# Router logits computed across in two column groups and turned back; scores of the diagonal chunk blocks alone

## The reference, cut to what matters

```python
scores = jnp.einsum('bhncd,bhnsd->bhncs', q_dec, k_inv)   # inside one chunk of 64
causal = jnp.tril(jnp.ones((CHUNK, CHUNK), dtype=bool))
scores = jnp.where(causal, scores, 0.0)
o_intra = jnp.einsum('bhncs,bhnse->bhnce', scores, vh)
```

```python
group_p = jax.nn.softmax((ht @ w_rg).astype(f32) + b_rg.astype(f32), axis=-1)
e_logit = ((ht @ w_re).astype(f32) + b_re.astype(f32)).reshape(T, N_GROUPS, EXPERTS_PER_GROUP)
```

## Time and profile before

| | |
|---|---|
| median of 3 runs | 1662.14 us (1656.52 to 1665.27) |
| the profiled execution's own time | 1662.17 us |
| its span in the profile | 1660.4 us |
| PE, PEld busy | 1520.1 us (92%), 1106.6 us (67%) |
| DVE, ACT, POOL busy | 1210.6 us (73%), 876.0 us (53%), 367.1 us (22%) |
| granted TensorE clock, mean | 0.954 of full speed |

### The profile page before, as it was taken

One profiled execution on the slowest core, in us unless ns is written; L12 is line 12 of the kernel. 1 busy time (PEld: TensorE's weight loads), 2 busy tenths in 40 slices (PEclk: granted clock), 3 DMA queues, 4 the chain that ended last, 5 costly groups with the idle time before them and its releaser, 6 DMA issues. The chain is left out here.

```text
span 1660.4 us, 23932 instructions
## 1 busy us (share of the span) xinstructions
PE 1520.1 (92%) x7453; PEld 1106.6 (67%) x7455; DVE 1210.6 (73%) x1932; ACT 876.0 (53%) x1534; POOL 367.1 (22%) x396
## 2 busy tenths in 40 slices
PE   4899879999989999999999999658999999999974
PEld 2779754889755889666889565445676677766741
DVE  2587994597975598974698945576788878777837
ACT  3324362324574324563324533356788887878846
POOL 1000000000010000011000011123476667665640
PEclk8899979999999999999999998769999999999996
DMA  9452361332332323332321543469999998889859
GB/s 320 168 185 94 93 260 42 89 102 78 126 102 76 102 79 100 116 113 77 89 89 52 228 127 114 153 228 329 352 295 274 344 262 240 223 243 284 275 109 384
DMA packets 201445, 291.27 MB, mean 175 GB/s; under 512 B 10558, under 2 KB 158171, under 8 KB 201370
## 3 DMA queue, kind: packets, MB, share of 16 engines
q1 hardware_dynamic: 171840, 197.18, 34.8%
q0 software_dynamic: 29360, 92.99, 20.5%
q10 hardware_dynamic: 170, 0.10, 0.0%
HBM read 240.42 MB, written 59.26 MB: 180 GB/s over the span
## 5 line engine op out<-in xcount | busy, mean ns | idle before, releaser
L1038 DVE SCALAR_TENSOR_TENSOR cv<-late_rows,taps,cv 128x512 f32<-128x512 f32 x480 | 321.8, 746 | 0.0
L1962 DVE TENSOR_TENSOR w_rest<-wgu,w_high 128x1024 fp32r<-128x1024 f32 x192 | 233.8, 1221 | 88.9 <-ACT w_high L1885 85.5
L1885 ACT ACTIVATE w_high<-wgu 128x1024 fp32r x192 | 201.7, 1054 | 97.9 <-PE pgu L1830 75.9
L531 PE MATMUL bank<-wo,yT 128*128 128x512 f32 x512 | 226.5, 599 | 3.6 <-ACT hT L736 2.5
L488 PE MATMUL bank<-hT_high,tiles_operand 128*128 128x512 f32 x496 | 197.2, 398 | 1.1 <-DVE logits L1132 1.1
L489 PE MATMUL bank<-hT_operand,tiles_operand 128*128 128x512 f32 x496 | 196.6, 396 | 0.0
L490 PE MATMUL bank<-hT_high,win_operand 128*128 128x512 f32 x496 | 196.6, 396 | 0.0
L531 PEld LDWEIGHTS bank<-wo,yT 128*128 128x128 f32 x512 | 96.7, 192 | 119.7 <-issue 117.7
L1840 PE MATMUL py<-wd,hTe 128*128 x384 | 172.7, 592 | 1.8 <-DVE hTe L1985 0.9
L1828 PE MATMUL pgu<-w_high,x_high 128*128 128x512 f32 x384 | 156.8, 408 | 3.8 <-DVE x_rest L1977 3.8
L1016 DVE TENSOR_TENSOR win_operand<-win,tiles_operand 128x2048 fp32r<-128x2048 f32 x48 | 109.9, 2290 | 58.1 <-ACT tiles_operand L758 58.0
(11 more groups left out here) (389 smaller groups left out, 2846.7 us busy)
## 6 DMA issues: line engine op xcount, KB each, us to landing
win<-w_in_in SPq DMA_DIRECT2D x64, 512.0 KB, 5.2
wgu<-w_gate_in SPq DMA_DIRECT2D x32, 1024.0 KB
wgu<-w_up_in SPq DMA_DIRECT2D x32, 1024.0 KB
wd<-w_down_in SPq DMA_DIRECT2D x32, 1024.0 KB
win<-w_in_in SPq DMA_DIRECT2D x16, 1024.0 KB, 5.1
wo<-w_ada_in POOLq DMA_DIRECT2D x6, 2048.0 KB, 11.2
y_dram<-zeros POOLq DMA_DIRECT2D x17, 512.0 KB, 5.1
tiles<-x_in POOLq DMA_DIRECT2D x16, 512.0 KB, 6.0
```

Source lines behind the costliest of these rows:

```text
L531: last = nc.tensor.matmul(out[:], yT[:, w % 2, k, :], wo[:, k, half * 512:(half + 1) * 512], start=(k == 0), stop=(k == KD - 1))
L1038: ins = V.scalar_tensor_tensor(out=cv[:, j], in0=u[:, j, w:w + T], scalar=tap, in1=cv[:, j], op0=ALU.mult, op1=ALU.add)
L1885: A(w_high[:, QK * q:QK * q + QK, :], c.wgu[:, bass.ds(slot, 1), QK * q:QK * q + QK, :].rearrange("p a k n -> p (a k) n"), ACT.Copy).then_ ...
L1962: V.tensor_tensor(w_rest[:, part, :], c.wgu[:, bass.ds(slot, 1), part, :].rearrange("p a k n -> p (a k) n"), w_high[:, part, :].bitcast(F3 ...
```

## The change

Logits of the tiles w = 2, 3 of block 0, all four of blocks 1 and 2, and w = 0, 1 of block 3 (`across`, 12 of 16 tiles): the router columns become stationary (36 columns) and the token tile moving (128 columns). The eight products alternate between two column groups, so that even k sum up in partitions 0 to 35 of the bank and odd k in partitions 64 to 99. A new ACT step `lsave` copies these 100 x 128 values back to `yt`, and a new PE step `lt` multiplies them, stationary, with a 0/1 matrix of 128 x 36 (`both_rows`), which adds the two halves and turns them to one row per token. DVE's `logit` now waits for `lt`. `both_rows` is made once, in the last tile's slot of `c.logits`, with one more DVE operation in `gains`; `cond_wide` moves by 8 columns for it.

Scores: in place of four products of 128 by 128, eight of 64 by 64, one per head and chunk, in two column groups. The semaphore `score_ready` now counts two per tile.

Lists: `lt` and `lsave` are put in. On PE at the end of blocks 0 to 2, `("r", 3)` goes from behind `("piece", 0)` to in front of it, with `("lt", 2)` between them. On DVE `("x1norm", 3)` goes in front of `("logit", 2)`. On ACT, `("turned", 2)` and `lsave` go in front of `("split", 1)`.

```diff
+        both_rows = c.logits[:, NTILES - 1, :]
+        across = lambda t, w: t < NB - 1 or t == NB - 1 and w < 2
...
             def logits(t, i):
                 pe.wait_ge(rin_ready, 2 * tile_no(t, i) + 2)
                 out = take("l", i, 0, t)
+                if across(t, i):
+                    for k in range(KD):
+                        at = k % 2 * CH
+                        last = nc.tensor.matmul(out[at:at + NR, 0:P], c.wroute[:, k, :], yt[:, i % 2, k * P:(k + 1) * P],
+                                                start=k < 2, stop=k >= KD - 2, skip_group_check=True)
+                        if k >= KD - 2:
+                            last.then_inc(logit_rows, 1)
+                    return
...
+            def turn_logits(t, i):
+                pe.wait_ge(logit_rows_saved, across_before(t, i) + 1)
+                out = place("l", i, 0, t)
+                nc.tensor.matmul(out[:, 0:NR], yt[:, i % 2, 0:P], both_rows, start=True, stop=True).then_inc(logit_ready, 1)
...
                 for h in range(NH):
-                    last = nc.tensor.matmul(pS[:, h * P:(h + 1) * P], ki[:, h, tok], qd[:, h, tok], start=True, stop=True)
-                last.then_inc(score_ready, 1)
+                    for s in range(2):
+                        a, b = i * P + s * CH, h * P + s * CH
+                        last = nc.tensor.matmul(pS[s * CH:(s + 1) * CH, b:b + CH], ki[:, h, a:a + CH], qd[:, h, a:a + CH],
+                                                start=True, stop=True, skip_group_check=True)
+                        if h == NH - 1:
+                            last.then_inc(score_ready, 1)
...
-                     ("y", 3, 0), ("A", 3), ("y", 3, 1), ("B", 3), ("r", 2), ("O", 3), ("l", 2), ("piece", 0),
-                     ("r", 3), ("oT", 2), ("oT", 3), ("l", 3), ("piece", 1)]
+                     ("y", 3, 0), ("A", 3), ("y", 3, 1), ("B", 3), ("r", 2), ("O", 3), ("l", 2), ("r", 3), ("lt", 2), ("piece", 0),
+                     ("oT", 2), ("l", 3), ("oT", 3), ("lt", 3), ("piece", 1)]
...
+            def save_logit_rows(t, w):
+                act.wait_ge(logit_rows, 2 * across_before(t, w) + 2)
+                A(yt[0:CH + NR, w % 2, 0:P], place("l", w, 0, t)[0:CH + NR, 0:P], ACT.Copy).then_inc(logit_rows_saved, 1)
...
-                     ("osq", 3), ("orstd", 3), ("rin", 3), ("split", 1), ("turned", 2), ("turned", 3)]
+                     ("osq", 3), ("orstd", 3), ("rin", 3), ("turned", 2), ("lsave", 3), ("split", 1), ("turned", 3)]
...
-                     ("logit", 2), ("x1norm", 3), ("oms", 3), ("state", 3, 1), ("gateo", 3), ("logit", 3),
+                     ("x1norm", 3), ("logit", 2), ("oms", 3), ("state", 3, 1), ("gateo", 3), ("logit", 3),
```

More of the change, by code:

```diff
@@ L248, in present @@
             return t < NB
-        TILE_WORK = ("y", "r", "l", "ysum", "x1sum", "rin", "ynorm", "x1norm", "logit")
+        TILE_WORK = ("y", "r", "l", "lt", "lsave", "ysum", "x1sum", "rin", "ynorm", "x1norm", "logit")
         NEXT_WORK = ("T", "piece", "xsum", "raw", "high", "split", "xnorm", "input", "rest")
@@ L680, in steps @@
                     else:
-                        {"y": y_half, "r": router_turn, "l": logits, "mean": mean, "var": variance, "A": scores, "B": state_sums,
+                        {"y": y_half, "r": router_turn, "l": logits, "lt": turn_logits, "mean": mean, "var": variance, "A": scores, "B": state_sums,
                          "O": outputs, "oT": turn_outputs}[kind](t, *at)
@@ L913, in _ @@
                      ("high", 2), ("key", 3), ("high", 3), ("x1sum", 2), ("osq", 2), ("ysum", 3), ("rin", 2),
-                     ("x1sum", 3), ("orstd", 2), ("osq", 3), ("orstd", 3), ("rin", 3), ("turned", 2), ("split", 1),
-                     ("turned", 3)]
+                     ("x1sum", 3), ("orstd", 2), ("lsave", 2), ("osq", 3), ("orstd", 3), ("rin", 3), ("turned", 2), ("lsave", 3),
+                     ("split", 1), ("turned", 3)]
             MIDDLE = [("ln", 0), ("xsum", 0), ("xsum", 1), ("ln", 1), ("ln", 2), ("raw", 0), ("end", 0), ("exps", 0), ("xsum", 2),
@@ L919, in _ @@
                      ("end", 3), ("gate",), ("key", 0), ("x1sum", 0), ("ysum", 1), ("key", 1), ("rin", 0), ("osq", 0),
-                     ("high", 0), ("orstd", 0), ("x1sum", 1), ("key", 2), ("turned", 0), ("rin", 1), ("osq", 1),
-                     ("high", 1), ("orstd", 1), ("high", 2), ("split", 0), ("turned", 1), ("ysum", 2), ("x1sum", 2),
-                     ("high", 3), ("osq", 2), ("key", 3), ("orstd", 2), ("ysum", 3), ("rin", 2), ("x1sum", 3),
-                     ("osq", 3), ("orstd", 3), ("rin", 3), ("split", 1), ("turned", 2), ("turned", 3)]
+                     ("high", 0), ("orstd", 0), ("x1sum", 1), ("lsave", 0), ("key", 2), ("turned", 0), ("rin", 1), ("osq", 1),
+                     ("high", 1), ("lsave", 1), ("orstd", 1), ("high", 2), ("split", 0), ("turned", 1), ("ysum", 2), ("x1sum", 2),
+                     ("high", 3), ("osq", 2), ("key", 3), ("orstd", 2), ("ysum", 3), ("rin", 2), ("x1sum", 3), ("lsave", 2),
+                     ("osq", 3), ("orstd", 3), ("rin", 3), ("turned", 2), ("lsave", 3), ("split", 1), ("turned", 3)]
             FINAL = [("ln", 0), ("ln", 1), ("ln", 2), ("end", 0), ("exps", 0), ("sq", 0), ("sq", 1), ("sq", 2), ("sq", 3),
@@ L926, in _ @@
                      ("end", 3), ("gate",), ("key", 0), ("x1sum", 0), ("ysum", 1), ("key", 1), ("rin", 0), ("osq", 0),
-                     ("orstd", 0), ("x1sum", 1), ("key", 2), ("turned", 0), ("rin", 1), ("osq", 1), ("orstd", 1),
+                     ("orstd", 0), ("x1sum", 1), ("lsave", 0), ("key", 2), ("turned", 0), ("rin", 1), ("osq", 1), ("lsave", 1), ("orstd", 1),
                      ("turned", 1), ("ysum", 2), ("x1sum", 2), ("osq", 2), ("key", 3), ("orstd", 2), ("ysum", 3),
@@ L941, in steps @@
                         {"ln": log_forget, "exps": head_exps, "end": end_exp, "sq": squares, "var": variance, "gate": conv_gate,
-                         "ysum": y_sums, "x1sum": x1_sums, "rin": router_in, "key": save_keys, "osq": square_outputs,
+                         "ysum": y_sums, "x1sum": x1_sums, "rin": router_in, "lsave": save_logit_rows, "key": save_keys, "osq": square_outputs,
                          "orstd": outputs_rstd, "turned": save_turned}[kind](t, *at)
@@ L1152, in mask @@
             def mask(t, i):
-                dve.wait_ge(score_ready, t * NT + i + 1)
+                dve.wait_ge(score_ready, 2 * (t * NT + i + 1))
                 V.copy_predicated(c.scoreT[:, i % 2].rearrange("p (h n) -> p h n", h=NH),
@@ L1202, in _ @@
                      ("x1norm", 2), ("bcopy",), ("place", 2), ("oms", 2), ("place", 3), ("mask", 3), ("state", 3, 0),
-                     ("input", 3), ("ynorm", 3), ("logit", 2), ("state", 3, 1), ("x1norm", 3), ("osave", 3),
+                     ("input", 3), ("ynorm", 3), ("state", 3, 1), ("x1norm", 3), ("logit", 2), ("osave", 3),
                      ("gateo", 2), ("oms", 3), ("gateo", 3), ("rest", 1), ("logit", 3)]
@@ L1267, in gains @@
                     mod_chain.step(V.tensor_copy(c.grow[:, r * 512:(r + 1) * 512], bank[r][:]))
+                mod_chain.step(V.tensor_tensor(both_rows, c.ident[:, 0:NR], c.ident[:, CH:CH + NR], ALU.add))
                 dve.wait_ge(row_done, 3)
```

4 lines of the change are left out of this document (3 added, 1 removed), and 8 rows, old and new, of tables (FINAL, FIRST, MIDDLE).

## The result

The changed kernel takes 1670.77 us (median of 7 runs, 1670.10 to 1672.46), the kernel before, measured beside it, 1660.46 us (7 runs, 1655.88 to 1665.27): ratio 1.0061 [1.0048, 1.0073], so 10.3 us slower.

What follows compares the result with a forecast made beforehand. PE, busy 92% of the span, was taken as the bound, each new idle moment paid in full. Terms 3.5 + 2.9 - 0.75 - 0.7 = +4.9 us, +10.9 with the clock, gave 1673 us; range 1660 to 1681.

Steps and rivals of the forecast that it cites:

- Its signs: In the trace after: PE idle 2.5 to 4 us before `r` 3, clock 0.50 behind, scores at 0.7 to 0.9 us.
- Logits product: On PE: 1.81 us falls to 1.0, `lt` adds 0.22; net 0.6 us saved per tile where PE is waited for.
- End of blocks 1 and 2: From `l` 2 to piece 1: PE stalls 2.67 us for `r` 3; piece 1 1.74 us later, twice, +3.5 us.
- End of block 0: Same way with block 0's rows: stall 3.81 us, piece 1 at 308.90 instead of 306.02, +2.9 us.
- Middle: Blocks 1 to 3: `l` 0's saving becomes a wait, `logit` 0 1.0 us late; -0.25 us a block, -0.75 for three.
- Scores: Scores product, 0.89 us before: 0.1 us saved in each of 7 places, 0.7 us saved, ends +2.0 and -1.3.
- Clock: Half-speed stretches behind the three new stalls at block ends: 2.0 us each, +6.0 us; 0 if the clock stays up.
- The code's part: Sum of all terms without the clock: 3.5 + 2.9 - 0.75 - 0.7 = +4.9 us.
- The rival without a stall: Block ends: `xn_ready` of tile 3 comes before `l` 2 is over, no stall, no clock drop; -4.2 us, 1658 us; 12%.

Runs made afterwards that it cites:

- `filled`: The changed kernel plus unread products of 512 columns ahead of `r` 3, four in block 0, three in blocks 1 and 2: 1666.71 us, ratio 1.0041 to before.
- `changed_again`: The changed kernel as it is, run once more: 1669.82 us, ratio 1.0051 to the kernel before.
- `stall_alone`: The kernel before with only `r` 3 moved ahead of piece 0 and `x1norm` 3 ahead of `logit` 2: 1670.67 us, ratio 1.0054 to before.
- `turn_behind`: The changed kernel with `r` 3 back behind piece 0, `lsave` 2 ahead of `x1sum` 3, `logit` 2 ahead of `x1norm` 3: 1660.99 us, ratio 0.9995 to before.
- `block0_filled`: `odd_bank` plus unread products of 128 columns ahead of waits in block 0: 1651.47 us, ratio 0.9945 to the kernel before.
- `odd_bank`: The changed kernel with logits in bank 1 or 3, `r` 3 then `lt` 2 behind piece 0, `logit` 2 behind `gateo` 3: 1652.80 us, ratio 0.9947 to before.

## Why the prediction was right

Forecast +10.9 us, measured +10.3, by the mechanism that it named. Its signs came, with two exceptions: the clock stayed at 1.00 behind one of the three stalls (block 1), and a scores step took 0.62 us and not 0.7 to 0.9. Term by term:

- **Logits product.** 1.0 us forecast, 1.00 measured: eight pairs at 0.11 and some 0.1 for leaving the split array. Right; the two column groups work side by side.
- **End of blocks 1 and 2.** Stall 2.67 forecast, 2.69 measured; `r` 3 0.93 for 0.87; the wait for `logit` 2 0.38 for 0.37. From piece 0 to piece 1 7.94 for 8.13: ACT's copy took 0.26 us, not 0.45, and no wait was left ahead of `lt` 3. Sum +1.60 us (13.29 - 11.69) for +1.74.
- **End of block 0.** Stall 3.83 for 3.81. The end with the clock up is seen in `filled`: block 0 is 112.71 - 109.94 = +2.8 us there with the same half-speed time as before; forecast +2.9.
- **Middle.** The wait ahead of the outputs came (1.14 us for some 0.9), so did `logit` 0's late start (0.90 us for 1.0). A whole block 1 or 2, free of half-speed time, is +1.1 us; the steps' terms add up to 1.74 - 0.25 - 0.1 (two scores places at most 0.2) = +1.3 to +1.4.
- **Scores.** 0.1 us a place forecast, 0.18 measured at the place shown, 0.25 us for a whole block, and nothing in the time. The term was too small to matter either way. The Trainium skill, page TensorE: Matmul & The Clock Gate, Part 3, has weight loads overlap with running products only when the row group differs, by which the scores would have been at their slow end. The trace does not bear that out: both column groups share their rows, and eight pairs took 0.62 us, 0.08 each, less than the 0.11 of a pair with 128 moving columns.
- **Clock.** 2.0 us for each of three stalls forecast, from stretches of 3.3 and 10.1 us taken at half their length. In the ledger before has 45.9 us at half speed, after 58.9 and, run again, 58.8: 13 us more, at 0.42 us each 5.4 us, for 6.0. The sum was right and its places were not: behind the stalls it was 6.8, 0 and 6.8 us in one execution and 3.4 us behind each of the three in the other. That 6.0 was met so closely is luck in part. In the three executions with such stalls (after, `changed_again`, `stall_alone`) eight of nine stalls had a half-speed stretch behind them; of the same places in before, `turn_behind` and `filled`, where PE had no such stall, none did. So the idle time is what does it, though not every time.

The code's part, with 2.8 for block 0, 1.1 twice and -0.3 for block 3 up to its third logits product, is +4.7 us for the +4.9 forecast. With the clock's 5.4 that makes 10.1, near the 10.3 of the medians; the profiled execution is only 8.5 us longer, because its block 3 came out 1.0 us shorter behind that product with no less time at half speed, which stays unexplained. The rival without a stall was closest to what could have been: `turn_behind`, which has none, came out level and not at -4.2, for two short waits at each block end took the stall's place, one of them for the same bank, and the scores brought less than they had been given. What the prediction did not look for is that this bank stood in the way of the order that pays.

## What to carry to other kernels

A cheaper product needs a place where PE is what is waited for; moving a step ahead of a long one to make room for it trades a hidden dependency for a stall, and in eight of nine such stalls here PE paid twice, once in the stall's length and once in clock. Price the move by the end of the releasing engine's operation, before pricing the product. When a wait goes back to a shared PSUM bank, try another bank before another order: here two lines for the bank, with `r` 3 in its old place and `lt` 2 and `logit` 2 moved back, turned +10 us into -8.8.

## What had not been expected of the hardware

- Going into a split array costs 0.09 us ahead of the first product, as coming back does behind the last.
- A stretch of 3.4 us at half speed cost 1.4 us of time, not 1.7. That part of it is hand-overs and other engines' work, which the clock doesn't touch, would explain this and is not shown.
- Filling one wait with products that nobody reads kept the clock at 1.00 there, and the clock fell behind other waits that after has too, where they had cost no clock (`filled`). Small products of 128 columns kept the clock up as well (`block0_filled`, 0.87 to 0.95).
- `odd_bank`'s 6 runs lie within 1.0 us, the 17 runs of before beside them within 6.6 us (1658.36 to 1664.99), and the 35 runs of before beside the last four kernels within 16 us (1650.68 to 1666.74). Half-speed stretches that differ from run to run fit: the mean clock of those 35 runs lies between 0.950 and 0.963, the three shortest (1650.68 to 1651.26) have 0.962 or 0.963, and the longest (1666.74) has 0.950. From 0.963 to 0.950 is some 43 us at half speed in a span of 1660 us, and the times differ by 0.3 to 0.4 us for each. Why the clock takes these ways is open.
